# Expert loop of a three-block kernel: one pass per expert and a ring of six weight halves released one by one

## What is computed

```python
g = xb @ w_gate[e] + b_gate[e]
u = xb @ w_up[e] + b_up[e]
g = jnp.minimum(g, 7.0)
u = jnp.clip(u, -7.0, 7.0)
act = g * jax.nn.sigmoid(1.702 * g) * (u + 1.0)
yb = act @ w_down[e] + b_down[e]
y = zeros.at[row_tok].add(yb * row_w[:, None])
```

## Time and profile before

| | us |
|---|---|
| median of three executions | 2554.79 |
| lowest, highest | 2546.99, 2555.33 |
| span of the profiled execution, first to last instruction | 2552.7 |
| PE busy | 2212.0 (87%) |
| PE weight loads busy | 1237.3 (48%) |
| DVE busy | 651.7 (26%) |
| ACT busy | 357.1 (14%) |
| mean of all DMA | 228 GB/s |

### The profile page before, as it was taken

How to read it: one execution, slowest core, us unless ns; L and a number is a source line. 1 busy time by engine, 2 the same in 40 slices (tenths; PEclk the granted TensorE clock), 3 DMA queues, 4 the chain that set the end, 5 groups by cost and what they waited for, 6 DMA issues and landing times.

```text
span 2552.7 us, 24185 instructions
## 1 busy us (share of the span) xinstructions
PE 2212.0 (87%) x9951; PEld 1237.3 (48%) x9952; DVE 651.7 (26%) x997; ACT 357.1 (14%) x548; POOL 103.9 (4%) x116
## 2 busy tenths in 40 slices
PE   6977789998899999999999797799979686858997
PEld 2643346333333333333333384488548475837873
DVE  2747623110111111111111115100016465420000
ACT  1211012111111111111111212100012221211000
POOL 1000010000000000000000100200000031200000
PEclk9888889999999999999999898899979887988999
DMA  9561155998699999969999741343333200013330
GB/s 346 207 230 50 66 192 204 398 428 359 263 427 428 427 428 428 428 262 413 428 427 417 290 163 65 83 151 146 133 130 132 99 1 1 1 67 116 139 109 17
DMA packets 106791, 580.77 MB, mean 228 GB/s; under 512 B 6992, under 2 KB 8084, under 8 KB 81969
## 3 DMA queue, kind: packets, MB, share of 16 engines
q1 hardware_dynamic: 101008, 562.40, 55.1%
q0 software_dynamic: 5696, 17.18, 2.2%
HBM read 578.49 MB, written 1.07 MB: 227 GB/s over the span
## 4 chain that ended last, share of the span: by engine, by line
PE 67%; DMA 16%; DVE 11%; ACT 3%; issue 2%; SPq 0%; DVEq 0%; POOL 0%; ACTq 0%
DMA ring<-in_w_up 14%; PE ps L1199 14%; PE ps L1586 12%; PE ps L1597 6%; PE ps L604 6%; PE ps L612 5%; PE ps L1214 5%; PE ps L516 1%; PE ps L1931 1%; PE ps L1222 1%; PE ps L1937 1%; DMA ring<-in_ada_w 1%; PE ps L825 1%; PE ps L1941 1%; PE ps L793 1%
## 5 line engine op out<-in xcount | busy, mean ns | idle before, releaser
L1199 PE MATMUL ps<-ring,arena 128*64 128x512 f32 x1632 | 362.6, 598 | 29.5 <-DMA ring<-in_w_up 23.5
L1586 PE MATMUL ps<-arena,ring 128*128 128x256 f32 x1408 | 308.2, 382 | 1.5 <-ACT arena L581 1.5
L1586 PEld LDWEIGHTS ps<-arena,ring 128*128 128x128 f32 x1408 | 270.0, 192 | 39.6 <-ACT arena L581 2.3
L1214 PE MATMUL ps<-ring,arena 128*64 128x512 f32 x1088 | 240.9, 594 | 9.0 <-ACT arena L1161 9.0
L1199 PEld LDWEIGHTS ps<-ring,arena 128*64 128x64 f32 x1632 | 114.7, 138 | 271.7 <-issue 231.2
L1134 DVE TENSOR_SCALAR arena<-ps 128x512 f32<-128x512 f32 x34 | 23.5, 692 | 546.3 <-PE ps L1199 546.3
L1214 PEld LDWEIGHTS ps<-ring,arena 128*64 128x64 f32 x1088 | 88.3, 137 | 139.1 <-issue 138.3
L1597 PE MATMUL ps<-ring,arena 128*128 128x512 f32 x352 | 151.4, 592 | 0.0
L604 PE MATMUL ps<-arena,ring 128*128 128x256 f32 x672 | 149.1, 384 | 0.7 <-ACT arena L581 0.7
L604 PEld LDWEIGHTS ps<-arena,ring 128*128 128x128 f32 x672 | 129.1, 193 | 20.4 <-issue 1.5
L1199 PE MATMUL ps<-arena 128*64 128x512 f32 x544 | 124.5, 611 | 11.2 <-issue 11.2
(11 more groups left out here) (453 smaller groups left out, 2147.5 us busy)
## 6 DMA issues: line engine op xcount, KB each, us to landing
ring<-in_w_up SPq DMA_DIRECT2D x64, 2048.0 KB, 17.3
ring<-in_w_down SPq DMA_DIRECT2D x64, 2048.0 KB, 16.2
ring<-in_w_gate SPq DMA_DIRECT2D x32, 2048.0 KB, 15.9
arena<-in_w_gate SPq DMA_DIRECT2D x32, 2048.0 KB, 15.9
ring<-in_ffn_w_gate_up SPq DMA_DIRECT2D x22, 2048.0 KB, 7.9
ring<-in_ada_w SPq DMA_DIRECT2D x12, 2048.0 KB, 17.7
ring<-in_ffn_w_down SPq DMA_DIRECT2D x10, 2048.0 KB, 7.7
ring<-in_w_in SPq DMA_DIRECT2D x8, 2048.0 KB, 18.0
```

The source lines that it names most:

```text
L1199: m = pe.matmul(bank(b)[c * CAP:(c + 1) * CAP, :], xT[:, j * P + h * CAP:j * P + (h + 1) * CAP], w[h][:, j, c * 512:(c + 1) * 512], start= ...
L1214: m = pe.matmul(bank(b)[d * CAP:(d + 1) * CAP, :], actT[:, j * P + h * CAP:j * P + (h + 1) * CAP], down_w[h][:, j, d * 512:(d + 1) * 512], ...
L1586: m = pe.matmul(bank(b0 + g)[:, c * SEQ:(c + 1) * SEQ], w[:, k, (2 * g + c) * P:(2 * g + c + 1) * P], hT2[:, k, :], start=(k == 0), stop=( ...
```

## The change

The two-expert body becomes one body per expert. The separate odd gate buffer goes; six halves lie in the ring in the order gate 0, up 0, gate 1, up 1, down 0, down 1, and each is released and loaded again by itself. A product function now does one half. The bias is opened at the start of an expert by two 64 x 128 matmuls instead of at the end of the one before by four of 32 x 64. The combine weights are made in the expert itself, between its first gate and up halves, not in the one before. In the large path both groups use a half before it is released. After the loop SP no longer waits for ff_ps and gain_in before it streams further pieces.

```diff
         def pe_narrow(pe, e, there):
             n = e + 1
             pe.wait_ge(main.x_ready, n * 2)
-            there(0)
-            pe_product(pe, gate_w[odd], XT, 0, main.g_ps)
-            there(1)
-            pe_product(pe, up_w, XT, 1, main.u_ps)
+            pe.wait_ge(main.e_ready, n)
+            pe_open(pe, 0)
+            for h in range(2):
+                there("g", h)
+                pe_product(pe, gate_w, h, XT, 0, main.g_ps)
+                if h == 0:
+                    pe_weights(pe, main, n)
+                there("u", h)
+                pe_product(pe, up_w, h, XT, 1, main.u_ps)
             pe_gather(pe, main, n + 1)
-            pe.wait_ge(main.a_ready, n * 2 - 1)
-            pe_weights(pe, main, n + 1)
-            pe_hidden(pe, main, n)
+            pe.wait_ge(main.pwT_ready, n)
             pe_gatherT(pe, main, n * 2 + 1)
-            there(2)
-            pe_down(pe, main, n, 2, main.d_ps)
-            pe.wait_ge(main.pwT_ready, n + 1)
-            pe_open(pe, 0, 1 - odd, 0)
-            pe_open(pe, 1, 1 - odd, 1)
-            pe_combine(pe, main, n, PwT[odd])
+            pe_hidden(pe, main, n, 0, act_)
+            there("d", 0)
+            pe.wait_ge(main.aT_ready, n)
+            pe_down(pe, 0, actT, 2, main.d_ps)
+            there("d", 1)
+            pe_down(pe, 1, actT, 2, main.d_ps)
+            pe_combine(pe, main, n, PwT, Yb)
...
         def pe_wide(pe, e, x, there):
...
+            pe.wait_ge(main.x_ready, n * 2)
+            pe.wait_ge(main.e_ready, n)
+            pe_open(pe, 0)
+            there("g", 0)
+            pe_product(pe, gate_w, 0, XT, 0, None)
             pe_gather(pe, extra, x)
+            pe_weights(pe, main, n)
+            there("u", 0)
+            pe_product(pe, up_w, 0, XT, 1, None)
+            pe.wait_ge(main.pwT_ready, n)
+            pe_gatherT(pe, extra, x * 2)
+            pe.wait_ge(extra.x_ready, x * 2 + 1)
+            pe_open(pe, 2)
+            pe_product(pe, gate_w, 0, XTf, 2, main.g_ps)
+            pe_product(pe, up_w, 0, XTf, 3, main.u_ps)
+            there("g", 1)
+            pe_product(pe, gate_w, 1, XT, 0, extra.g_ps)
+            pe_product(pe, gate_w, 1, XTf, 2, main.g_ps)
+            there("u", 1)
+            pe_product(pe, up_w, 1, XT, 1, extra.u_ps)
+            pe_product(pe, up_w, 1, XTf, 3, main.u_ps)
+            pe_hidden(pe, main, n, 0, act_)
+            pe_weights(pe, extra, x, 1)
+            there("d", 0)
+            pe.wait_ge(main.aT_ready, n)
+            pe_down(pe, 0, actT, 0, None)
+            pe_hidden(pe, extra, x, 2, actf)
+            pe.wait_ge(extra.aT_ready, x)
+            pe_down(pe, 0, actTf, 3, main.d_ps)
+            there("d", 1)
+            pe_down(pe, 1, actT, 0, extra.d_ps)
+            pe_down(pe, 1, actTf, 3, main.d_ps)
+            pe_gather(pe, main, n + 1)
+            pe_combine(pe, main, n, PwT, Yb)
             pe.wait_ge(extra.pwT_ready, x)
+            pe_gatherT(pe, main, n * 2 + 1, 1)
+            pe_combine(pe, extra, x, PwTf, Ybf)
...
         def act_narrow(act, e):
             n = e + 1
+            act_weights(act, main, n, PwT)
             act_sigmoid(act, main, n)
             act_gathered(act, main, n * 2 + 1)
-            act_weights(act, main, n + 1, PwT[1 - odd])
-            act_hidden(act, main, n)
             act_gatheredT(act, main, n * 2 + 2, XT)
-            act_out(act, main, (main.d_ps, n))
+            act_hidden(act, main, n, 0, actT)
+            act_out(act, main, (main.d_ps, n * 2), 2, Yb)
...
+        def pe_open(pe, b):
+            for i in range(2):
+                pe.matmul(bank(b + i), E64[i * CAP:(i + 1) * CAP, :], bgu[i * CAP:(i + 1) * CAP, :], start=True, stop=False,
+                          tile_position=(i * CAP, 0), skip_group_check=True)
...
         def sp_s7(sp):
+            for i in range(SLOTS):
+                used = pieces[FIRST - SLOTS + i]
+                sp.wait_ge(used[1], used[2])
+                load_in(sp, i, 0)
+            with sp.Fori(0, E - 1) as e:
+                for i, (done, nth) in enumerate(((main.g_ps, 1), (main.u_ps, 1), (main.g_ps, 2), (main.u_ps, 2), (main.d_ps, 1), (main.d_ps, 2))):
+                    sp.wait_ge(done, e * 2 + nth)
+                    load_in(sp, i, e + 1)
...
             sp_s7(sp)
-            stream(sp, LAST, LAST + 2)
-            sp.wait_ge(ff_ps, 1)
-            sp.wait_ge(gain_in, 32)
-            stream(sp, LAST + 2, len(pieces))
+            stream(sp, LAST, len(pieces))
```

More of the change, by code:

```diff
@@ L20 @@
 E, TOPK, CAP = 32, 4, 64
+FEW = CAP // 2
 ROUNDS = SEQ // CAP
@@ L1186, in pe_weights @@
             m.then_inc(s.pwT_ps, 1)
[L1188 to L1201, removed]
@@ L1203, in pe_hidden, with pe_product @@
-        def pe_hidden(pe, s, n):
+        def pe_open(pe, b):
+            for i in range(2):
+                pe.matmul(bank(b + i), E64[i * CAP:(i + 1) * CAP, :], bgu[i * CAP:(i + 1) * CAP, :], start=True, stop=False,
+                          tile_position=(i * CAP, 0), skip_group_check=True)
+        def pe_product(pe, w, h, xT, b, done):
+            for j in range(4):
+                for c in range(2):
+                    m = pe.matmul(bank(b)[c * CAP:(c + 1) * CAP, :], xT[:, j * P + h * CAP:j * P + (h + 1) * CAP],
+                                  w[h][:, j, c * 512:(c + 1) * 512], start=False, stop=(h + j == 4), skip_group_check=True)
+            if done is not None:
+                m.then_inc(done, 1)
@@ L1204, in pe_hidden @@
+        def pe_hidden(pe, s, n, b, of):
             pe.wait_ge(s.a_ready, n * 2)
             for j in range(4):
-                m = pe.transpose(bank(0)[:, j * P:(j + 1) * P], every4(act_, j), ident)
+                m = pe.transpose(bank(b)[:, j * P:(j + 1) * P], every4(of, j), ident)
             m.then_inc(s.aT_ps, 1)
[L1209 to L1216, removed]
@@ L1218, in pe_combine, with pe_down @@
-        def pe_combine(pe, s, n, pwT):
+        def pe_down(pe, h, aT, b, done):
+            for j in range(4):
+                for d in range(2):
+                    m = pe.matmul(bank(b)[d * CAP:(d + 1) * CAP, :], aT[:, j * P + h * CAP:j * P + (h + 1) * CAP],
+                                  down_w[h][:, j, d * 512:(d + 1) * 512], start=(h + j == 0), stop=(h + j == 4))
+            if done is not None:
+                m.then_inc(done, 1)
+        def pe_combine(pe, s, n, pwT, y):
+            pe.wait_ge(s.pwT_ready, n)
@@ L1356, in expert_rounds @@
             eng.reg_mov(rounds, 0)
[L1357 to L1368 removed]
+            with eng.Fori(0, E) as e:
+                n_e = eng.value_load(cnt[0:1, bass.ds(e, 1)], min_val=0, max_val=SEQ)
+                if first is not None:
+                    first(e)
+                fork = nc.cur_bb
+                eng.br_cond(n_e > CAP, f"large_{which}", f"small_{which}")
+                nc.switch_bb(f"small_{which}", parent=fork)
+                narrow(e)
+                eng.br(f"next_{which}")
+                nc.switch_bb(f"next_{which}", parent=fork)
             def large():
@@ L1391, in pe_s7, with there, weights @@
         def pe_s7(pe):
-            def there(i, e, odd):
-                def weights(n):
-                    for h in range(2):
-                        if n == 0:
-                            ready, before = (odd_ready[h], 0) if odd else (slot_ready[E_SLOT[h]], E_USED[h])
-                            pe.wait_ge(ready, i * 16 + 16 * (before + 1))
-                        else:
-                            pe.wait_ge(slot_ready[E_SLOT[2 * n + h]], e * 16 + 16 * (E_USED[2 * n + h] + 1))
+            def there(e):
+                def weights(what, h):
+                    i = {"g": (0, 2), "u": (1, 3), "d": (4, 5)}[what][h]
+                    pe.wait_ge(slot_ready[E_SLOT[i]], e * 16 + 16 * (E_USED[i] + 1))
@@ L1416, in act_s7 @@
         def act_s7(act):
             act_gathered(act, main, 1)
-            act_weights(act, main, 1, PwT[0])
             act_gatheredT(act, main, 2, XT)
-            return expert_rounds(act, lambda i, e, odd: act_narrow(act, e, odd), lambda i, e, odd, x: act_wide(act, e, odd, x),
-                          lambda i, e, odd, r, x: act_further(act, x))
-        def load_in(sp, name, e, odd=0):
-            i = ("w_gate", "w_up", "w_down").index(name)
-            w = A[name][0][e:e + 1] if isinstance(e, int) else A[name][0][bass.ds(e, 1)]
-            for h in range(2):
-                dst = (gate_w[odd], up_w, down_w)[i][h]
-                there = odd_ready[h] if i == 0 and odd else slot_ready[E_SLOT[2 * i + h]]
-                src = w[:, h * 512:(h + 1) * 512, :].rearrange("a (p k) n -> p (a k n)", p=P)
-                sp.dma_start(dst.rearrange("p k n -> p (k n)"), src).then_inc(there, 16)
@@ L1433, in sp_s7 @@
-        def sp_s7(sp):
-            for i, name in enumerate(("w_gate", "w_up", "w_down")):
-                if name == "w_down":
-                    sp.wait_ge(router_ps, 2)
-                    load_in(sp, "w_gate", 1, 1)
```

(18 more changed lines are left out.)

246 lines of the change are left out of this document (108 added, 138 removed).

## The result

The changed kernel takes 2577.51 us (median of four executions, 2574.79 to 2579.29) beside 2555.06 for the kernel before: ratio 1.0089, 95% interval 1.0071 to 1.0107. It is slower by 0.9%, where 2583 was forecast. Its profiled execution has a span of 2576.0 us, 23.3 more than before.

A forecast was written before the change was run, and what follows sets the result against it. PE's chain per expert was taken to bound the loop, with 28.0 us lost to late weights. 2552.7 + 54.3 + 2.2 - 28.0 - 0.4 = 2580.8 span, median 2.1 above: 2583 us, range 2545 to 2602.

The forecast's parts named there:

- What bounds: Expert loop: PE loses 28.0 us to late weights, the most better load order returns; PE's chain per expert counts 30 times.
- Loads: Weight stream in the loop: halves released singly leave some 19 us of slack, so all 28.0 us of waits go.
- the faster rival: Small experts: ACT's copies are overlapped, period stays near 27.8 us; 2527 with both returns free; chance 0.15.
- The tail before down: Small expert, gather to down: gathered transposes now first, two ACT copies no longer hidden, +0.66 us.
- The weights between products: Small expert: combine weights' transposes now stand between two products instead of filling the tail, +0.47 us.
- Open and combine: Small expert, down to next product: combine waits for ACT's copy, then 1.92 and the open's 0.86 us, +0.68 us.
- rival 4: Much slower: open's two matmuls don't overlap, 2610, or slot waits inside products interrupt PE, 2596; chance 0.06.
- Large experts: The two large experts: smaller opens -0.85, three uncovered ACT copies, sum +1.1 us each, +2.2 together.
- Branches: Large-path entries stay at 5.78 and 5.47 us, returns' sum unchanged at 7.15, with bounds of -7.15 and +7.15.
- Rival 3: Large-path returns: both stall, everything else as forecast, 2590 us; chance 0.16.
- The start: Loop start: the first open waits for ACT's copy and begins at 441.67 against the old first product's 442.06, -0.4 us.
- Behind the loop: After the loop: next ring product follows an ACT copy, not a load, so earlier streaming brings and costs nothing.

The follow-up runs named there:

- e1: Changed kernel with hidden transposes put back before the gathered rows' transposes, on PE and ACT: 2558.75 us, ratio 1.0018.
- e4: Changed kernel, new ring kept, with hidden transposes first, the open ahead of the combine and the combine weights back in the tail: 2530.27 us, ratio 0.9922.
- e6: Changed kernel with SP reloading both halves of a matrix only when its second half is through: 2575.32 us, ratio 1.0110.
- e9: Changed kernel with the old SP gate (ff_ps, gain_in) behind the loop after two of the next block's pieces: 2577.16 us, ratio 1.0108.
- e8: Changed kernel with experts above 50 tokens, not 64, on the large path, five experts instead of two: 2668.03 us in one execution.
- e2: Changed kernel with the next expert's open moved back between down and combine, in its new form: 2550.16 us, ratio 0.9985.

## Why the prediction was right, point by point

**What bounds.** That the gain to be had was 28.0 us and that a small expert's chain weighs thirty times decided the sign. e1 to e4 show it directly: with the chain shortened in different steps, by 0.55, 0.84 and 1.07, the time falls by 19, 27 and 30 us, and with all of it, 1.90 a small expert, by 47.

**Loads.** No wait for weights was forecast and none occurred. The slack came out as 14 us in e4, where 19 had been computed, for the last half and not for the one that comes late (see e4). That makes no difference at 29.51 us, as e6 shows, but it does in e4, where eight experts wait and the faster rival's working had three.

**The tail before down**, forecast +0.66: gather to down is 550.82 - 546.25 = 4.57 us, where it was 4.03, so +0.54. The steps came as chained up to ACT's two copies, in its timeline:

```profile
549.61 0.59 ACT L1155 COPY arena<-ps 128x512 f32<-128x512 f32 x1 [0.84 <-PE ps L1185]
550.09 0.59 ACT L1167 COPY arena<-ps 128x512 f32<-128x512 f32 x1
```

They start 0.48 apart and overlap, where I had put one behind the other, 0.59.

**The weights between products**, +0.47: the first half with what follows takes 535.90 - 531.95 = 3.95, against 16 x 0.215 = 3.44 for sixteen records: +0.51.

**Open and combine**, +0.68: from down to the next product 561.45 - 550.82 = 10.63, before 9.95: +0.68. The sum fits better than its terms: the open adds 0.98 instead of 0.86, the combine 560.47 - 558.68 = 1.79 instead of 1.92. The open is far from the 1.72 of two matmuls one after the other, so rival 4's first form is out. Its second, interruptions at the slot waits, is out too: 48 records across three halves take 10.35 us (535.90 to 546.25), 0.216 each.

Together 1.75 us measured, 1.81 forecast: over 30 experts 52.5 instead of 54.3.

**Large experts**, +2.2 in all: measured 58.90 + 56.98 against 58.29 + 58.07, -0.5. The second one wasn't preceded by a stall, so its first product ran at full pace. Between the two, 1.9 us are that. In the kernel before both had a slow first product, 9.80 and 9.66 where 7.09 is usual. Without it they are 55.6 and 55.5 us, and the second one of the changed kernel, 56.98, is about 1.4 longer where 1.1 was forecast. So the work did grow as forecast, and the missing stall hid it.

**Branches**, forecast unchanged at 18.4: 5.88 + 5.88 and 2.2 behind the return (31.69 us from open to open at 690.34, over 29.51) are 13.9, -4.5. This is the term that was sized worst. I had assumed that both entries stall; the second did not. Rival 3, both returns stalling, didn't occur either: one did. And e9, with the same program on PE, stalled at both entries and the second return. So this term could not be had from one trace of the kernel before, and how near it came is partly chance.

**The start**, -0.4: the first product began 0.7 us earlier and took 2.1 us longer (5.72 for its 16 records, elsewhere 3.65). PE's clock was low there. From 441 to 445 us, first in the changed kernel and then in e9, which has the same program on PE (columns as in the last section):

```profile
441.00:445.00 4.00, 4.00 (x12) 1.18 (x12) 0.00 (x0) 0.14 (x1) 0.00 (x0) 0.50 0.00 0
```

```profile
441.00:445.00 4.00, 4.00 (x20) 1.20 (x19) 0.00 (x0) 1.28 (x1) 0.00 (x0) 1.00 0.00 0
```

The granted clock is 0.50 in the one and 1.00 in the other, where the first product takes 3.65. With 0.9 less for the open that the last expert no longer has behind it this is +1.2. In sum 52.5 - 28.0 - 0.5 - 4.5 + 1.2 = 20.7, and 21.0 were measured in the loop.

**Behind the loop**, nothing: e9 confirms that the streaming has no part in it.

**How near.** For the loop, 54.3 + 2.2 - 28.0 - 0.4 = 28.1 us were forecast and 21.0 measured, 7.1 less. Outside it nothing was forecast and 2.3 more were measured, which I ascribe to nothing. So the total came nearer to the forecast than the loop did, and that is luck. The sign and the terms of the small expert are not.

The faster rival was right in its mechanism and wrong about this kernel. It needed the copies to be covered; e4 covers them, down to the 0.29 us before down that the kernel before has too, and lands at 2530, where the rival had 2527 with no stalls at the returns; e4 had one.

## What to carry to other kernels

Count what each engine hands over between two matmuls before the order is changed: with the ACT copies of 0.59 us no longer hidden behind transposes and bias matmuls, tail and combine grew by 0.54 + 0.68 us an expert, some 37 us over 30, more than the 28 that all waits for weights had cost. Where two limits are within a few per cent (here 27.8 and 29.4 us), buffers only pay if the compute chain stays under the stream, and a longer chain only costs if it doesn't: judge both together, in one period. And two changes that come in one edit are worth running apart, since the good half of this one, the ring of single halves, was hidden by the other.

## What the runs showed of the hardware

Jumps between the loop and the code behind the program cost PE 3.6 to 6.4 us or nothing, and neither place nor sequence told which: in the changed kernel the first entry and return stalled and the second pair did not; e4 stalled at both entries and one return (5.6, 5.6 and 4.9 us); in e8 four of its crossings did. The Trainium skill (Runtime: NRT & Kernel Launch, section Instruction fetch mechanics) has a jump out of the fetched window pay for a fetch. That agrees with the stalls, and leaves the free crossings unexplained; PE's own program doesn't decide it alone: e6 and e9 both have that of the changed kernel, and e6 stalled where it did, e9 elsewhere. Whether it varies between executions of one kernel or with the place in memory wasn't tried; one execution of each kernel was traced.

The two 64 x 128 matmuls of the open (four records), in different row halves, added 0.96 to 0.98 us together (525.53 to 526.50 in e2). And what follows such a stall is slower: from the starts 690.34, 692.34 and 697.09 in the changed kernel, the open took 2.00 us and the half product 4.75, against 0.98 and 3.58 elsewhere. The window that holds a stall has a mean granted clock of 0.95, so part of it was at the lower of the two levels; the one without is at 1.00, all of it at 2.4 GHz. Behind the return's stall (third and fourth row) it is 0.50, the lower level of 1.2 GHz, and then 0.66:

```profile
618.00:684.00 66.00, 58.22 (x260) 20.22 (x256) 7.97 (x17) 8.87 (x14) 0.00 (x0) 0.95 0.63 243
1105.00:1163.00 58.00, 55.84 (x258) 19.70 (x256) 8.00 (x17) 8.87 (x14) 0.00 (x0) 1.00 0.72 276
688.00:692.00 4.00, 1.66 (x4) 0.53 (x4) 0.00 (x0) 1.28 (x1) 0.00 (x0) 0.50 0.02 6
692.00:696.00 4.00, 4.00 (x14) 1.19 (x14) 0.00 (x0) 0.00 (x0) 0.00 (x0) 0.66 0.00 0
```

The first two rows are the windows around the two large experts of the changed kernel, the others stretches behind the first return: stretch, its length, busy time and count of PE, PEld, DVE, ACT and POOL, then PE's granted clock, the DMA share and GB/s.
